# A hybrid decoder step on eight cores: one weight load moved ahead of four row loads, and four row scalings moved from ScalarE to VectorE

## The reference, cut to what matters

```python
def layer(x, ...):
    h = rmsnorm(x, norm_g)
    proj = einsum('btd,de->bte', h, w_in)        # five blocks of 512: a_in | a_gate | u | v | b_gate
    a_out = pool_mix(a_in) * silu(a_gate)        # trailing means, a 128x128 map per channel group
    vn = rmsnorm(v per head of 128, v_norm_g)
    b_out = u * (tril(w_s) @ vn + b_s) * silu(b_gate)     # per chunk of 128 rows
    return x + concat(a_out, b_out) @ w_out      # w_out is 1024 x 1024
```

## Time and profile before

| what | us |
|---|---|
| median of 3 timed runs | 455.48 (455.07 to 455.79) |
| the profiled execution, its own time | 454.13 |
| its span on the slowest core (core 3) | 452.6 |
| spans of all cores | 450.7 to 452.6 |
| PE busy on core 3 | 427.7 (95%) |
| DVE / ACT / POOL busy on core 3 | 304.3 / 176.3 / 146.4 |

### The profile page before, as it was taken

How to read it: one execution, slowest core, us unless ns; L and a number is a source line. 1 busy time by engine, 2 the same in 40 slices (tenths; PEclk the granted TensorE clock), 3 DMA queues, 4 the chain that set the end, 5 groups by cost and what they waited for, 6 DMA issues and landing times.

```text
span 452.6 us, 7818 instructions; the slowest of 8 cores (450.7 to 452.6 us)
## 1 busy us (share of the span) xinstructions
PE 427.7 (95%) x2375; PEld 197.8 (44%) x2375; DVE 304.3 (67%) x650; ACT 176.3 (39%) x297; POOL 146.4 (32%) x241
## 2 busy tenths in 40 slices
PE   2989989999999999999999999999999999999990
PEld 1434445444444444444444444444444444444440
DVE  1666736667985677867586766767666655867665
ACT  2434144374124813348132841137313642324063
POOL 8454002610044554641047262171005200470000
PEclk9999999999999999999999999999999999999996
DMA  7999999990608833720646004010130004310013
GB/s 200 171 169 168 225 252 199 176 159 19 89 6 157 161 60 86 252 76 2 89 149 230 4 4 94 1 30 3 30 65 2 1 1 93 140 70 5 1 74 113
DMA packets 35833, 43.28 MB, mean 96 GB/s; under 512 B 27256, under 2 KB 27888, under 8 KB 34224
## 3 DMA queue, kind: packets, MB, share of 16 engines
q0 software_dynamic: 4288, 20.45, 23.9%
q1 hardware_dynamic: 5296, 14.88, 10.3%
q10 hardware_dynamic: 26208, 7.45, 8.9%
HBM read 42.19 MB, written 10.09 MB: 116 GB/s over the span
## 4 chain that ended last, share of the span: by engine, by line
PE 89%; ACT 3%; DVE 2%; DMA 2%; issue 1%; POOL 1%; ACTq 0%; another core or an unknown queue 0%; DVEq 0%; POOLq 0%
PE pF L543 59%; PE pF L1088 22%; DMA xg<-x 2%; PE pF L1058 2%; PE pF L1020 2%; ACT vscr L833 1%; PE pT L573 1%; PE pT L510 1%; DVE xg L1097 1%; PE pF L573 1%; ACT hT L881 1%; PE pF L1049 1%; DVE vn_sb L644 0%; PE pF L460 0%; PE pT L672 0%
## 5 line engine op out<-in xcount | busy, mean ns | idle before, releaser
L543 PE MATMUL pF<-hT,win 128*128 128x512 bf16 x1024 | 231.3, 379 | 1.5 <-DVE vn_sb L644 1.3
L543 PEld LDWEIGHTS pF<-hT,win 128*128 128x128 bf16 x1024 | 98.6, 98 | 117.2 <-issue 3.7
L1088 PE MATMUL pF<-wout,mix 128*128 128x512 bf16 (+1 forms) x520 | 113.5, 376 | 1.5 <-DMA wout<-wout_h 1.3
L1088 PEld LDWEIGHTS pF<-wout,mix 128*128 128x128 bf16 x520 | 50.0, 98 | 60.2 <-issue 3.4
L1097 DVE TENSOR_TENSOR xg<-pF,xg 128x512 f32<-128x512 f32 (+1 forms) x65 | 44.3, 682 | 31.8 <-PE pF L1088 29.9
L543 PE MATMUL pF<-win,hT 128*128 128x512 bf16 x256 | 56.8, 379 | 0.0
L488 ACT ACTIVATE vscr<-xg 128x1024 bf16<-128x1024 f32 x40 | 42.2, 1056 | 37.0 <-DVE xg L1097 24.7
L500 ACT ACTIVATE hb<-xg,ssx 128x1024 bf16<-128x1024 f32 x28 | 30.7, 1141 | 59.5 <-PE pF L1088 55.7
L451 POOL TENSOR_SCALAR ssx<-ssx 128x1 f32<-128x1 f32 (+3 forms) x24 | 9.7, 403 | 135.4 <-ACT vscr L488 127.4
L629 ACT ACTIVATE vscr<-pF 128x512 f32<-128x512 f32 x32 | 19.1, 597 | 70.6 <-PE pF L543 57.9
L451 POOL TENSOR_SCALAR ss<-ss 128x4 f32<-128x4 f32 (+1 forms) x34 | 10.4, 307 | 96.7 <-DVE ss L632 96.3
(11 more groups left out here) (113 smaller groups left out, 347.4 us busy)
## 6 DMA issues: line engine op xcount, KB each, us to landing
win<-win_h POOLq DMA_DIRECT2D x8, 1024.0 KB, 45.6
y<-xg SPq DMA_DIRECT2D x12, 512.0 KB, 3.1
xg<-x SPq DMA_DIRECT2D x9, 512.0 KB, 5.5
wout<-wout_h POOLq DMA_DIRECT2D x4, 1024.0 KB, 33.3
xg<-x POOLq DMA_DIRECT2D x7, 512.0 KB, 47.5
win<-win_h POOLq DMA_DIRECT2D x4, 256.0 KB, 13.7
win<-win_h POOLq DMA_DIRECT2D x2, 512.0 KB, 19.9
y<-hT SPq DMA_DIRECT2D x4, 256.0 KB, 2.1
```

The lines of the kernel that those rows point to most:

```text
L543: r = h.matmul(out=out_ap, lhsT=lhsT(k), rhs=rhs(k), start=(k == 0), stop=(k == 7))
L1088: r = h.matmul(out=pf[:, 0:w], lhsT=mix[:, k, i * 128:(i + 1) * 128], rhs=wout[l][:, hf, k, c0:c0 + w], start=(k == 0), stop=(k == 7))
```

## The change

Three edits:

- The load of the second half of layer 0's output weights is issued ahead of the loads of tiles 4 and 5, directly behind the first half. Tiles 4 to 7 follow it.
- At `n == 0` the four squares and factors of group 1 stand ahead of all output products (each tile's factor by itself). The scaling of its rows is `scale_v`, a VectorE `tensor_scalar`, in place of `scale` on ScalarE, and stands later: tile 0's behind the sixth output product's addition, tile 1's behind the first `norm_tr`, tiles 2 and 3 behind the second `norm_tr`. The first two `norm_tr` stand behind the seventh and the eighth output product.
- The `norm_tr` of tiles 2 and 3 move into the next item: ahead of the v products of its tiles 1 and 2.

```diff
         load_wout(0, (0,))
-        load_tile(4, eng=POOL)
-        load_tile(5, eng=POOL)
         load_wout(0, (1,))
-        load_tile(6, eng=POOL)
-        load_tile(7, eng=POOL)
+        for t in range(4, 8):
+            load_tile(t, eng=POOL)
...
+            def scale_v(self, i):
+                xa = xap(self.G, i)
+                c = self.c0 + i
+                S.emit(DVE, lambda h: h.tensor_scalar(out=hb[:, i % NHB, :], in0=xa, scalar1=rsx[:, c:c + 1], scalar2=None,
+                                                      op0=ALU.mult),
+                       reads=[xbuf(self.G, i), buf(f"rsx_{c}")], writes=[buf(f"hb{i % NHB}")])
...
             for i in range(TPG):
+                if n == 1 and i in (1, 2):
+                    norm_tr(G, l, i + 1)
                 pf, pfb = proj_tm(l, i, C_V, banks[i], last)
                 st2 = v_tile(G, l, i, pf, pfb)
                 if pend is not None:
...
             if n == 0:
-                nrm.square(0)
-                nrm.square(1)
-                nrm.rstd(0, 2)
-                nrm.scale(0)
-                nrm.scale(1)
+                for i in range(TPG):
+                    nrm.square(i)
+                    nrm.rstd(i, 1)
                 out_two((0, 0), (1, 0))
-                out_mm(2, 0)
-                out_mm(3, 0)
-                nrm.square(2)
-                nrm.rstd(2, 1)
-                nrm.scale(2)
-                nrm.square(3)
-                nrm.rstd(3, 1)
-                out_mm(0, 1)
+                for i, hf in ((2, 0), (3, 0), (0, 1), (1, 1)):
+                    out_mm(i, hf)
+                nrm.scale_v(0)
+                out_mm(2, 1)
                 norm_tr(*nx, 0)
-                nrm.scale(3)
+                nrm.scale_v(1)
+                out_mm(3, 1)
                 norm_tr(*nx, 1)
-                out_mm(1, 1)
-                out_mm(2, 1)
-                norm_tr(*nx, 2)
-                out_mm(3, 1)
-                norm_tr(*nx, 3)
+                nrm.scale_v(2)
+                nrm.scale_v(3)
                 return
```

## The result

The change makes the kernel slower. Seven runs of each on one chip gave a median of 458.64 us (457.39 to 460.05) against 455.85 us (455.07 to 457.11) for the kernel before: a ratio of 1.006 [1.0043, 1.0077]. A few executions run in a slower state, with a lower clock on the cores of a die; all medians, ratios and counts here are of the others. The profiled execution took 458.07 us, with 456.5 us on its slowest core, now core 5. Of the two cores that the sum followed, core 0 came out at 455.6 (455.7 was worked out) and core 3 at 455.5 (454.5 was).

A forecast was written before the change was run, and what follows sets the result against it. TensorE's queue was taken to bound the kernel. Core 0 lost 3.4 us and core 3 lost 3.4 less 1.48, putting the slowest 3.1 higher: 455.48 + 3.1 = 458.6, stated as 458.5 us, range 456.2 to 459.9.

The forecast's parts named there:

- the unhindered 22.5 us: TensorE's time without gaps from the first output product to the last v product, claimed to be 22.5 us.
- No slack: Claim that TensorE, busy 344.47 of 345.00 us from 82 us on, passes earlier gains or losses undiminished to the end.
- The wait of 1.18 us: TensorE's stand for the second half of the output weights; its removal was to gain 1.48 us on core 3, nothing on core 0.
- the scalings gain nothing by leaving ScalarE: Four scalings of 1.15 us each on ScalarE were held to be off the chain, so moving them gains nothing.
- 0.68, 0.49 and 1.76: Forecast TensorE gaps in us ahead of transposes 1, transposes 2 and the fourth v product; with restarts, a 3.4 us loss.
- +3.1 us for the slowest core: Forecast rise of the slowest core, from 452.6 on core 3 to 455.7 on core 0.
- the 457.2 worked out for it: Forecast time in us of the profiled execution, 3.1 above the 454.13 of the kernel before.
- the 1.35 that was carried over: The timed median's 1.35 us excess over the profiled execution of the kernel before, assumed to hold after the change.
- the wait for weights was longer in the timed runs: Rival: weights come later on every core, so more wait goes; 456.1 us at 11%, or 454.4 us at 5%.
- VectorE's queue did hold the last v product: Opposing rival: the queue does not hold it, leaving two gaps and 1.5 us loss; 456.7 us, chance 4%.
- Rows weren't late: Opposing rival: SP's loads delay tile 4 by up to 1.0 us, so scaling 0 waits 0.4; 459.0 us, chance 5%.
- The clock did not fall behind these gaps: Opposing rival: TensorE's clock falls in the gaps, the 32 v products taking 6.8 us more; 465 us, chance 3%.

The follow-up runs named there:

- e5: Changed kernel with scalings back on ScalarE and each moved transposition directly behind a v product, leaving no gaps: 454.66 us, ratio 1.0009 to the kernel before.
- e3: Changed kernel with tile 3's transposition emitted behind the second v product, so its hT multiplication precedes reduction 1 and v_scale 0: 455.38 us, ratio 1.0033.
- e7: Changed kernel with each of the four VectorE scalings emitted twice: 460.64 us, ratio 1.0131 to the kernel before.
- e4: e3 with the four scalings back on ScalarE, between the squares: 455.61 us, ratio 1.0022 to the kernel before.
- e0: The changed kernel run again unaltered, on a second chip: 456.58 us, ratio 1.006 to the kernel before.
- e2: Changed kernel with the loads in their old order: 457.31 us, ratio 1.0073 to the kernel before.
- e6: e5 with the loads in their old order: 454.78 us, ratio 1.0006 to the kernel before.
- e1: Kernel before with only the load of the second half of the output weights moved ahead of tiles 4 and 5: 456.74 us, ratio 1.0067.
- e8: Kernel before with six unused matmuls filling TensorE's wait for the a_gate weights around 32 us: 453.79 us, ratio 0.9986.
- e9: e5 with six unused matmuls filling TensorE's wait for the a_gate weights around 32 us: 453.32 us, ratio 0.9979 to the kernel before.

## Why the prediction was right

**What bounds the kernel.** TensorE's queue: held, and the unhindered 22.5 us are e5's stage on eight cores (22.67 by the timeline, which starts its first row 0.16 us earlier). "No slack" behind the change was a little too strict. The 0.53 us that are missing in the earlier trace rows are a wait of TensorE for GpSimd at 267 us, a row of core 3 that has no such wait in the changed kernel (below it):

```profile
267.84 0.24 PE L672 MATMUL pT<-ident,smpb 16*128 16x16 bf16 x4 [0.53 <-POOL smpb L722]
...
270.75 0.25 PE L677 MATMUL pT<-ident,smpb 16*128 16x16 bf16 x4
```

Seven cores of the kernel before wait there for 0.38 to 0.54 us; in the changed kernel no core waits more than 0.23. So some of the loss is won back behind the stage. Why GpSimd holds TensorE up less there is not shown.

**The load.** The wait of 1.18 us went; no core of the changed kernel has one. On core 3 the half was there by 62.0 us, where 62.4 was worked out: the first small load on SP, which stands behind it, started at 65.55 before and at 62.01 after.

```profile
65.55 0.34 SPq L368 DMA_DIRECT2D smp<-xs  x1
...
62.01 0.34 SPq L366 DMA_DIRECT2D smp<-xs  x1
```

Rows were never late for VectorE: on core 2 of the changed kernel, where the scaling of tile 0 had the least to spare of the eight cores, its factor was there at 65.72 and its scaling started at 67.81. That the scalings gain nothing by leaving ScalarE was right for the cores followed, not for all: on core 2 of the kernel before the last transposes waited for one, and this wait is gone too.

```profile
72.50 0.61 PE L510 MATMUL pT<-ident,hb 128*128 128x128 bf16 x8 [0.54 <-ACT hb L500]
```

Otherwise the squares, factors and scalings taken off ScalarE gave and cost nothing that shows.

**The gaps.** In the chain of core 5 they are 0.61, 0.40 and 1.72 us where 0.68, 0.49 and 1.76 were worked out, each with a restart of 0.16; the stage is 3.25 us longer than an unhindered one, for 3.4. The scaling is why the terms were a little large; line 498 on core 5 (least, median and most ns, first and last start):

```profile
L498 DVE TENSOR_SCALAR hb<-xg,ssx x4: 742/744/749, 71.5 to 77.8; 128x1024 bf16<-128x1024 f32 x4
```

It took 0.744 us where 0.80 was assumed, just below the least of the earlier trace rows. The Trainium skill ("VectorE: DVE Perf Modes", section "The TRN2 errata") led to an estimate of 0.59; the measurement is a quarter above it and decides. (With 0.59 in its place the prediction's own steps give a loss of 3.0 us, not the 2.9 that it names.) e3 shows that the last gap, half the loss, is the queue order, and e7 that it doesn't grow with the scalings; e4 and e7 together show that the first two are the scalings.

**The sum.** +3.1 us for the slowest core: +2.79 by the medians here, 456.58 - 454.31 = +2.27 on the second chip. The working was a little high, by 0.15 us in the stage and by what is won back behind it: cores 4 to 7 need 370.3 to 370.7 us from the last v product to their end, where they needed 370.9 to 371.2 before. Cores 0 to 3 need 371.5 to 371.7, for 370.8 to 371.3, because of something that was not in the sum. From about 95 to 102 us all four cores of their die were granted 0.81 of the clock, with TensorE busy throughout; core 0 and, below it, core 4 of the other die (length, busy time, clock, DMA share, GB/s):

```profile
96.00:100.00 4.00, 4.00 (x17) 1.69 (x16) 3.08 (x6) 3.97 (x8) 0.00 (x0) 0.81 1.07 166
...
96.00:100.00 4.00, 4.00 (x20) 1.82 (x19) 3.56 (x8) 4.00 (x9) 0.00 (x0) 1.00 1.01 172
```

By estimate this costs about 6.5 x 0.19 = 1.2 us. It came more than ten microseconds behind the last gap, and no other kept trace has it; e0 and e2, with the same gaps, do not. So it was luck that core 0 came out within 0.1 us: it began the stage 0.36 us earlier, lost 3.26 for 3.4 in it, and needed 0.4 more behind it. The median was helped by luck too. The profiled execution took 0.9 us more than the 457.2 worked out for it, since core 5 began its stage at 60.24 (58.42 before), behind a fall of the clock at 36 us, and the median lay 0.57 us above that execution, not the 1.35 that was carried over. What the 1.35 us were is not settled; runs of the kernel before differ among themselves by 2 us here.

**The rivals.** That the wait for weights was longer in the timed runs fell with e2, e5 and e6: with or without the new order the time is the same within about 1 us, and that rival needed a wait of 2.8 us or more. VectorE's queue did hold the last v product. Rows weren't late. The clock did not fall behind these gaps, but it did behind stands of 1.87 and 2.08 us in e1, hardly longer than the last gap, and behind the earlier one in the kernel before, so that rival was closer than the argument from the tail made it look.

**What it missed.** The prediction took the slowest core from one profiled execution, core 3, whose last place came with the wait. Over many runs the slowest core is in more than half of them one with the low mean clock, and e8 and e9 put most of these down to the stand at 32 us. The number wasn't hurt, since the gaps hit all cores alike and the wait was priced at 0.3 us at most. That the new load order makes such falls more frequent is not shown: on the second chip e5 had 19 such spans of 96, e6 with the old order 17 of 96, e0 with the new order 10 of 96, and the kernel before 30 of 216.

## What to carry to other kernels

Where one engine is busy without a break behind a change, write out the queue of the engine that feeds it, operation by operation, from the last product that is not affected: three gaps came out to within 0.1 us, and the largest of them had nothing to do with the scalings, only with what stands ahead of the last `hT` multiplication in its new place. A wait that a profile shows on some cores is worth only what it costs the core that is last; where the slowest core counts, ask first over many runs which core that is. A stage measured on all eight cores tells variants apart to 0.01 us where no wait differs from core to core, as in e3, e4 and e5; what it gains need not reach the total, as e4 shows.

## What the runs showed of the hardware

Behind stands of about 2 to 4 us the granted clock of TensorE fell to the lower of its two levels (0.50 of full speed, 1.2 of 2.4 GHz), on some cores and not on others with the same kind of stand: 2.55 us on core 5 of the kernel before was followed by about three microseconds at half speed, 2.76 us on core 7 of the changed kernel by none, and the 1.73 us gap of the changed kernel by none on any core. In e1 a stand of 1.87 us was followed by such a fall on core 5, one of 2.17 us on core 7 was not. Six idle matmuls in the stand took the share of core spans with a mean clock of 0.988 or less from 16% to 4% and 1%. Apart from stands, in the profiled execution of the changed kernel all four cores of one die were granted 0.81 for about 6.5 us while TensorE was busy throughout; the other die kept 1.00, and no other kept trace shows it.
